# Sample attention of a hybrid layer: key pages turned in 32x32 blocks on VectorE, all of them in the stretch of prompt attention, values in the delta rule

## The chip, the cores and the metric

One core of one Trainium2 chip runs the whole program. The metric is the device time of one execution in microseconds. Fp32 data throughout; large weight matmuls are made of three matmuls of rounded parts.

## The reference

One layer of a macaron transformer (half a feed-forward, token mixing, half a feed-forward, adaLN modulation) for a prompt of 256 tokens and for 8 sequences of 4 new tokens that each have 2048 past tokens in a paged cache. Token mixing adds two head groups on the same input: a gated delta rule (4 heads of 128) and block attention (8 heads of 64). What the change touches is the attention of the new tokens and the order in which it stands beside the delta rule:

```python
def moba_sample(q, k, v, cache_k, cache_v, page_table):
    past = page_table.shape[1] * PAGE_SIZE          # 16 pages of 128
    ppb = MOBA_BLOCK // PAGE_SIZE                   # 2 pages to a block
    j = past // MOBA_BLOCK                          # 8 blocks
    l_own = own_block_logits(q, k_own, t, ..., slopes)
    k_full = cache_k[page_table[:, : j * ppb]].reshape(b, j, MOBA_BLOCK, h, hd)
    kmean = jnp.mean(k_full.astype(jnp.float32), axis=2)
    gate = jnp.einsum("bqhd,bnhd->bqhn", q.astype(jnp.float32), kmean)
    _, idx = lax.top_k(gate, 3)                     # per query and head
    ...
    l_sel = selected_logits(q, k_sel, t, idx, slopes)
    return attend_merged(l_sel, v_sel, l_own, v_own)   # one softmax over 3 blocks and the own 4 tokens
```

The kernel makes the logits of all 8 blocks, because different queries and heads choose different blocks, gets the gate from their sums, and sets the logits of unchosen blocks so low that their probabilities are 0. All 128 key pages and 128 value pages (256 KB each) are read.

## The kernel before, in words

Each engine has a program of its own, with semaphores between them; an engine runs its instructions in the written order, so the order in the text is the schedule. After the projections (`w_in`, 29 turns of a PSUM bank) the kernel runs:

- a short preparation: K and V rows of the tokens are transposed for the outputs, the block-diagonal queries `Qbd` built by ScalarE, the logits of the own tokens made (L972);
- **the key stretch**, 64 steps over `m`. The 8 sequences go in two halves `g`; a unit `n` is one block of 256 keys of four sequences, so 16 units, and `m = 4n + c` takes feature chunk `c`. Per step TensorE transposes 8 pieces of 128x128 (helper line L704) into two banks, ScalarE copies one bank (L1465), VectorE the other (L1855), and one step later four matmuls make logits (L1015). VectorE adds the bias and takes sums and maxima (L1795 to L1798). Between the steps, once a unit, stands one turn of prompt attention (`attention(s)`, one head a turn: scores, bias, maximum, exponential, transposes, values), and later the squares, sums and inverse roots of the delta rule's queries and keys;
- **the delta rule** in 128-token chunks, 9 problems (8 of the prompt, one for all new tokens): an opening (cumulated decays, rows, decay matrix `DT`, transposed keys `KB`, `KDc` and values `VB`, Gram matrices), seven levels of the triangular inverse (`P`, `XP`, `PX`, L1187, L1196, L1200) with the sample steps between them (`sample(l)`, L1161 for the products with the recurrent states `st`), then the last chain `W`, `U0`, `S1`, `V1`, `o0`, `o1`, `S2`, and the norm sums `rms`. At each of 17 places `values(n)` puts in one block of value pages of four sequences: probabilities (ScalarE), two transposes (L704), a copy (L1847) and 8 matmuls of 512 columns (L1055); own tokens L1061, gathering into the mixed input L1069. VectorE does nearly all PSUM copies of this part, the level masks (L1933) and the masking by decay. ScalarE issues the loads of the states (L1515) when the key stretch is over;
- the output projection (L1251) from `wo`, two halves of W_out.

Pages go through `page`: a table entry is loaded into a register (L533) and one DMA is issued (L534), half the pages by SP and half by POOL. Slots: 12 units of key pages (8 in `kv`, 4 in the last slot of `wring`), four quads of value pages in `kv`. The slots of `wring` hold weight tiles before and the delta rule's buffers during this time. W_out goes to `kv` when the last values but one are read (L607 to L610).

## Time and profile before

| | us |
|---|---|
| median of 3 runs (lowest, highest) | 928.0 (927.4, 933.94) |
| profiled execution | 927.22 |
| its span on the core | 925.6 |
| TensorE busy in the span | 859.5 |
| VectorE, ScalarE, POOL busy | 501.3, 304.6, 113.9 |

How to read it: a row of a stage or window gives the stretch, its length, then for PE (TensorE matmul), PEld (its weight loads), DVE (VectorE), ACT (ScalarE) and POOL the busy time and the number of instructions, then the granted TensorE clock as a share of full speed, the mean busy share of the 16 DMA engines and GB/s. A group row gives line, engine, operation, output and input with shapes, the count, busy time and mean ns of one, then the idle time before them and what ended it. Two records stand for one fp32 matmul and one for a transpose. A fp32 matmul pipelines with the next, so means of one are longer than the step between starts. A timeline row gives start, length and the merged instructions.

### The profile page before, as it was taken

Reading aid. Unit: us, or ns where it says so; the run is one execution under the profiler, and the core shown is the slowest. Engines: PE = TensorE matmul, PEld = TensorE weight load, DVE = VectorE, ACT = ScalarE, POOL = GpSimd, SP = SyncE. Lnnn points to the kernel's source line nnn. Section 1 sums busy time; section 2 is a strip of 40 time slices with the busy share of each in tenths; the row PEclk is TensorE's granted clock in tenths of the full one; section 3 lists DMA queues with packets and bytes.
Section 4 is the critical chain, followed back from the end, with each engine's and each line's share of the span. In section 5 each row is a group of like instructions: output and inputs, shape, how many; then the busy total and the mean of one; then the engine's idle time right before and its main releaser. Section 6 shows DMA issues by size and latency. Waiting matters only on the chain.

```text
span 925.6 us, 19660 instructions
## 1 busy us (share of the span) xinstructions
PE 859.5 (93%) x7464; PEld 751.7 (81%) x7464; DVE 501.3 (54%) x961; ACT 304.6 (33%) x499; POOL 113.9 (12%) x197
## 2 busy tenths in 40 slices
PE   4889999999999999999999848998899999999996
PEld 3789999998997999966656524665777999999996
DVE  1445454543355667566656566657446565544363
ACT  1333333332323336453434511000225334432331
POOL 2000000000021000132223223230130000000021
PEclk9999999999999999999999988999999999999999
DMA  9999979785755252378778698898391555434401
GB/s 323 370 307 357 308 255 312 253 320 185 300 199 182 92 182 59 125 243 268 230 232 289 205 369 289 296 333 311 87 338 57 167 182 176 145 137 156 159 1 51
DMA packets 122163, 204.83 MB, mean 221 GB/s; under 512 B 7548, under 2 KB 56982, under 8 KB 121970
## 3 DMA queue, kind: packets, MB, share of 16 engines
q1 hardware_dynamic: 104976, 163.08, 50.9%
q0 software_dynamic: 11648, 38.45, 12.4%
q10 hardware_dynamic: 5474, 2.39, 1.0%
q8 instruction: 46, 0.75, 0.3%
q14 instruction: 19, 0.16, 0.1%
HBM read 199.01 MB, written 4.88 MB: 220 GB/s over the span
## 4 chain that ended last, share of the span: by engine, by line
PE 83%; DVE 5%; DMA 4%; issue 2%; ACTq 2%; ACT 2%; POOL 1%; POOLq 1%; DVEq 0%; SPq 0%
PE bank L741 19%; PE bank L743 18%; PE bank L742 18%; PE bank L704 8%; PE bank L1015 3%; PE bank L1251 3%; PE bank L723 3%; PE bank L1055 2%; DMA kv<-in_cache_v 2%; ACTq L1515 2%; DMA wring<-in_w_ada 1%; DMA region<-in_x_sample 1%; DVE wring_rounded L1590 1%; PE bank L1200 1%; PE bank L1187 1%
## 5 line engine op out<-in xcount | busy, mean ns | idle before, releaser
L741 PE MATMUL bank<-hn_rounded,kv_rounded 128*128 128x288 f32 x928 | 276.7, 298 | 5.9 <-DVE wring_rounded L1590 4.1
L742 PE MATMUL bank<-xs_rounded,kv_rounded 128*128 128x288 f32 x928 | 274.4, 296 | 0.0
L743 PE MATMUL bank<-hn_rounded,wring_rounded 128*128 128x288 f32 x928 | 273.6, 295 | 0.0
L1590 DVE TENSOR_TENSOR wring_rounded<-wring,kv_rounded 128x1024 fp32r<-128x1024 f32 (+1 forms) x164 | 188.3, 1198 | 71.7 <-ACT kv_rounded L1311 71.6
L1311 ACT CAST kv_rounded<-wring 128x1024 fp32r<-128x1024 f32 (+1 forms) x164 | 158.5, 1026 | 162.0 <-PE bank L743 109.7
L741 PEld LDWEIGHTS bank<-hn_rounded,kv_rounded 128*128 128x128 f32 x928 | 174.4, 188 | 10.2 <-DVE wring_rounded L1590 4.7
L743 PEld LDWEIGHTS bank<-hn_rounded,wring_rounded 128*128 128x128 f32 x928 | 175.4, 189 | 0.0
L742 PEld LDWEIGHTS bank<-xs_rounded,kv_rounded 128*128 128x128 f32 x928 | 174.9, 189 | 0.0
L741 PE MATMUL bank<-region_rounded,kv_rounded 128*128 128x288 f32 x352 | 105.5, 300 | 1.6 <-DVE modT L1582 1.6
L742 PE MATMUL bank<-region_rounded,kv_rounded 128*128 128x288 f32 x352 | 104.6, 297 | 0.0
L743 PE MATMUL bank<-region_rounded,wring_rounded 128*128 128x288 f32 x352 | 104.2, 296 | 0.0
L1644 DVE TENSOR_TENSOR sgate<-sgate,bank 128x288 f32<-128x288 f32 x44 | 20.0, 454 | 131.1 <-PE bank L743 123.2
L741 PEld LDWEIGHTS bank<-region_rounded,kv_rounded 128*128 128x128 f32 x352 | 66.6, 189 | 2.4 <-DVE modT L1582 2.0
L743 PEld LDWEIGHTS bank<-region_rounded,wring_rounded 128*128 128x128 f32 x352 | 67.0, 190 | 0.0
L742 PEld LDWEIGHTS bank<-region_rounded,kv_rounded 128*128 128x128 f32 x352 | 66.8, 190 | 0.0
L1855 DVE COPY wring<-bank 128x512 f32<-128x512 f32 x64 | 44.1, 689 | 41.7 <-PE bank L704 40.7
L1465 ACT COPY wring<-bank 128x512 f32<-128x512 f32 x64 | 37.3, 584 | 70.4 <-PE bank L704 70.4
L1278 ACT ACTIVATE sgate<-bank 128x288 f32<-128x288 f32 x44 | 18.1, 412 | 104.5 <-PE bank L743 104.5
L704 PEld LDWEIGHTS bank<-const,kv 128*128 128x128 f32 x352 | 37.7, 141 | 17.3 <-ACT wring L1465 12.4
L704 PE MATMUL bank<-const,kv 128*128 128x128 f32 x352 | 47.9, 279 | 0.0
L641 POOL TENSOR_TENSOR xs<-h 128x288 f32<-128x288 f32 x21 | 14.0, 668 | 255.3 <-DVE h L1668 254.9
L534 POOL DMA_DIRECT2D kv<-in_cache_v x64 | 34.4, 537 | 84.5 <-issue 54.0
(275 smaller groups left out, 987.4 us busy)
## 6 DMA issues: line engine op xcount, KB each, us to landing
wring<-in_ffn_up SPq DMA_DIRECT2D x44, 1024.0 KB, 7.7
wring<-in_w_ada SPq DMA_DIRECT2D x36, 1024.0 KB, 10.9
wring<-in_ffn_down SPq DMA_DIRECT2D x16, 1024.0 KB, 7.3
kv<-in_cache_v SPq DMA_DIRECT2D x64, 256.0 KB, 4.9
kv<-in_cache_v POOLq DMA_DIRECT2D x64, 256.0 KB, 5.2
wring<-in_w_in SPq DMA_DIRECT2D x14, 1024.0 KB, 6.4
kv<-in_cache_k SPq DMA_DIRECT2D x44, 256.0 KB, 4.5
kv<-in_cache_k POOLq DMA_DIRECT2D x44, 256.0 KB, 4.8
```

The lines of the kernel that those rows point to most:

```text
L534: eng.dma_start(dst, cache[which][bass.ds(p, 1), :, :].rearrange("a p n -> (a p) n")).then_inc(landed, 16)
L704: return nc.tensor.transpose(out, in_, ident[0:n, 0:n])
L723: m = nc.tensor.matmul(out[32 * g:32 * g + 32, 0:P], cT[:, k, :], wring[:, slot, k, g * P:(g + 1) * P], start=(k == 0), stop=(k == KD - 1) ...
L741: nc.tensor.matmul(out, hi, rhs_hi, start=start, stop=False)
L742: nc.tensor.matmul(out, hi, rhs_lo, start=False, stop=False)
L743: return nc.tensor.matmul(out, lo, rhs_hi, start=False, stop=stop)
L1015: ins = mm(ps[4][32 * b4:32 * b4 + 32, 0:BLK], Qbd[:, c, 4 * (n // NBLK) + b4, :], ktb[:, c % 2, b4 // 2, (b4 % 2) * BLK:(b4 % 2 + 1) * BL ...
L1251: m = mm(ps[4 * (1 - g) + i][:, 0:TOK], wo[g][:, k, i * P:(i + 1) * P], mix[:, k, :], start=(k == 4), stop=(k == 3))
L1311: nc.scalar.copy(whiR[:, u % 2, c, :], wring[:, n % RING, c, :]).then_inc(s_whi, 1)
L1465: nc.scalar.copy(ktb[:, m % 2, 0, :], ps[2 * (m % 2)][:, :]).then_inc(s_ktA, 1)
L1590: v.tensor_tensor(wringR[:, slot, c, :], wring[:, slot, c, :], whiR[:, u % 2, c, :], ALU.subtract).then_inc(s_wlo, 1)
L1855: v.tensor_copy(ktb[:, m % 2, 1, :], ps[2 * (m % 2) + 1][:, :]).then_inc(s_ktD, 1)
```

## The change

- A **quad** is four pages of one sequence, 1 MB; there are 32 for keys and 32 for values. SP alone issues them, one table load for four entries. The first eight go to two free slots of `wring` and to `kv` as the projections release them, each later one into the slot of the quad four before it in `kv`.
- `keys_turned`: VectorE transposes a quad in place in 32x32 blocks. With query weights `W` laid out to match (a permuted spread of the queries by TensorE, masked per sequence by POOL), 16 matmuls give logits of one quad in a layout of head pair, key block, head and token on partitions. `logits_out`: ScalarE copies them from PSUM with block sums; POOL adds the bias, VectorE takes the block maxima. Gates and sums are added over partitions by a matmul with `same`.
- `transposed(b)`: 64 small matmuls with `pick` take the probabilities of one sequence, apart for both halves of the heads, and turn them; values are then 16 matmuls of 128 columns with 8 weight columns per quad.
- The order is a list of portions; all 32 key quads stand between the ten turns of prompt attention, four portions a turn, the value quads between steps of the delta rule, and the last five behind its norm sums.
- The delta rule's copies of rows, keys, and of the last chain go from VectorE to ScalarE, level masks, triangular mask, the products of queries and the clearing for the state products to POOL. Norms use one table of ScalarE (logarithm straight from PSUM).
- W_out goes to `wring` slots 0 and 1 behind the end of the delta rule; the tiles that come after it into these slots wait for its last readers. The bias constants shrink.

```python
# SP
+            for n in range(2 * QUADS):
+                if n < 8 and n % 2 == 0:
+                    sp.wait_ge(*released(("in", (3, 4, 5, 6)[n // 2])))
+                elif n >= 8:
+                    sp.wait_ge(*consumed(n - 4))
+                load_quad(n)        # one load of 4 table entries, 4 dma_starts of 256 KB
+            sp.wait_ge(s_gdn, 1)
+            for g in range(2):
                 for k in range(2):
                     sp.dma_start(wo[g][:, 4 * k:4 * k + 4, :], ...).then_inc(s_wo[g], 16)
-            first_k_steps(sp, 0); stream_rest(sp, 0)   # and the same on POOL
-            for g in (1, 0):
-                sp.wait_ge(s_PV, 32 - 2 * g)
# order of all engines
+        def portions():
+            out = []
+            for n in range(QUADS):
+                out.append(("K", n // NQ, n % NQ))
+                out += {17: [("G", 0)], 18: [("X", 0)], 20: [("X", 1)], 22: [("X", 2)], 24: [("X", 3)],
+                        26: [("R", 0)], 29: [("T", 0)], 31: [("T", 1)]}.get(n, [])
+            for n in range(QUADS):
+                b, q = n // NQ, n % NQ
+                out.append(("V", b, q))
+                if q == NQ - 1 and b + 2 < NB:
+                    out.append(("T", b + 2))
+                out += {1: [("G", 1)], 3: [("X", 4)], 5: [("X", 5)], 9: [("X", 6)], 13: [("X", 7)], 15: [("R", 1)]}.get(n, [])
+            return out + [("O", NB - 1)]
+        def turns(point):           # 4 portions at points 0 to 9, the rest over 10 to 33
+            def upto(i):
+                return 4 * i if i <= 10 else 40 + (len(PORTIONS) - 46) * (i - 10) // 23
# TensorE
+            def logits(b, q):
+                n = NQ * b + q
+                pe.wait_ge(s_X, n + 1)
...
+                for j in range(4):
+                    for c in range(4):
+                        m = mm(ps[5 + 2 * (b % 2)][32 * c:32 * c + 32, P * q:P * q + P], W[b % 2][:, j // 2, 2 * c + j % 2, :],
+                               keys[:, :, 4 * c + j, :], start=(j == 0), stop=(j == 3), tile_position=(0, 32 * c))
+            for s in range(HM + 2):
+                attention(s)
+                if s < 8:
+                    qk_sum(s)
+                attend(s)
# ScalarE, behind the key stretch
+            for part in (RSq, RSk):
+                fn(part, part, ACT.Exp, scale=-0.5).then_inc(s_rse, 1)
+            act.wait_ge(s_pav, 8)
             act.wait_ge(s_own, 1)
             for hh in range(HG):
                 act.dma_start(st[hh], a["state_gdn"][0, :, hh].rearrange("b k v -> k b v")).then_inc(s_st, 16)
# VectorE
+            def keys_turned(n):
+                dve.wait_ge(*quad_landed(n))
+                v.transpose(quad(n), quad(n)).then_inc(s_X, 1)
+            for s in range(HM + 2):
+                normalise(s)
+                biased(s)
...
+                attend(s)
```

## Rows read from the trace of the kernel before

**Rows 1.** Stages, 402.7 us to the output projection
```profile
402.70:529.40 126.70, 121.83 (x1116) 76.70 (x1115) 81.67 (x185) 57.85 (x126) 31.01 (x58) 1.00 0.73 238
529.40:566.70 37.30, 22.40 (x153) 11.56 (x153) 20.47 (x55) 5.63 (x15) 9.86 (x19) 0.82 0.96 324
566.70:664.50 97.80, 86.51 (x780) 61.19 (x776) 63.84 (x146) 7.65 (x21) 23.93 (x43) 0.98 0.75 266
```

**Rows 2.** Groups by line and shape, 402 to 530 us
```profile
L704 PE MATMUL bank<-const,kv 128*128 128x128 f32 x343 | 46.8, 279 | 0.0
...
L1855 DVE COPY wring<-bank 128x512 f32<-128x512 f32 x64 | 44.1, 689 | 41.7 <-PE bank L704 40.7
```

**Rows 3.** Waits of TensorE over the whole span
```profile
PE bank L704 <- ACT sgate L1278: 11.8, 1, 11.8
...
PE bank L704 <- ACT region L1278: 6.7, 1, 6.7
PE bank L1055 <- DMA kv<-in_cache_v: 6.7, 5, 2.4
```

**Rows 4.** ScalarE's queue in time, and its DMA queue, 530 to 665 us
```profile
540.82 11.50 ACTq L1515 DMA_DIRECT2D region<-in_state_gdn  x3
...
q10 hardware_dynamic: 4160, 2.10, 5.8%
```

**Rows 5.** Groups by line and shape, 402 to 530 us, nearest prices
```profile
L1780 DVE SCALAR_TENSOR_TENSOR wring<-const,bank 128x384 f32<-128x384 f32 x8 | 4.4, 554 | 1.3 <-PE bank L984 1.3
...
L1278 ACT ACTIVATE wring<-wring 128x128 f32<-128x128 f32 x8 | 3.3, 412 | 0.0
...
L1772 DVE TENSOR_SCALAR wring<-wring 128x256 f32<-128x256 f32 x8 | 2.8, 347 | 0.0
...
L1771 DVE TENSOR_SCALAR wring<-wring 128x128 f32<-128x128 f32 x8 | 2.3, 287 | 0.3
...
L1873 DVE COPY wring<-region 128x1152 f32<-128x1152 f32 x1 | 1.3, 1344 | 0.0
```

**Rows 6.** Timeline row (own logits) and line view (state matmuls)
```profile
399.35 1.49 PE L972 MATMUL bank<-region,adasb 128*32 128x32 f32 x64 [1.90 <-DVE wring L1759]
...
L1161 PE MATMUL bank<-region,wring x96: 272/273/297, 605.4 to 608.8; 128*32 128x128 f32 x96
```

**Rows 7.** Windows inside the opening and at level 0
```profile
536.00:546.00 10.00, 5.74 (x48) 2.68 (x44) 9.93 (x36) 1.87 (x5) 3.97 (x8) 1.00 1.02 370
546.00:556.00 10.00, 0.00 (x0) 0.00 (x0) 2.62 (x5) 0.10 (x1) 1.07 (x2) 0.53 1.07 358
...
576.00:578.50 2.50, 1.61 (x9) 0.28 (x9) 0.08 (x1) 0.00 (x0) 1.07 (x2) 0.76 1.01 396
```

**Rows 8.** SP's issues of the first four pages, 362 to 369 us
```profile
364.13 3.67 SPq L534 DMA_DIRECT2D wring<-in_cache_k  x4
...
L533 SPq TENSOR_LOAD <-ptab x4: 272/274/463, 363.2 to 366.8; - x4
...
L534 SPq DMA_DIRECT2D wring<-in_cache_k x4: 332/344/361, 364.1 to 367.5; - x4
```

**Rows 9.** Page slots by window; transposed probabilities, 529.4 to 664.4 us
```profile
566.70:664.50 97.80, 22.36 (x181) 4.45 (x177) 21.47 (x40) 0.98 0.75 266
...
L704 PE MATMUL bank<-const,sgate 128*128 128x128 f32 x30 | 6.1, 286 | 11.8 <-ACT sgate L1278 11.8
```

**Rows 10.** POOL's squares; VectorE's final scaling, its line view
```profile
L641 POOL TENSOR_TENSOR xs<-h 128x288 f32<-128x288 f32 x21 | 14.0, 668 | 255.3 <-DVE h L1668 254.9
...
L1671 DVE TENSOR_SCALAR hn<-h,pvec x8: 370/876/880, 885.8 to 917.1; 128x288 f32<-128x288 f32 x8
```

**Rows 11.** Loads of W_out, and the first projection matmul
```profile
L610 SPq DMA_DIRECT2D kv<-in_w_out x4: 368/448/508, 630.8 to 636.9; - x4
DMA to landing us min/median/max: 6.1/7.4/8.7
...
664.48 3.88 PE L1251 MATMUL bank<-hn,kv 128*128 128x288 f32 x15 [0.60 <-issue]
```

More of the change, by code:

```diff
@@ L527, in squared @@
+        PORTIONS = portions()
+        POINTS = 33
+        def turns(point):
+            def upto(i):
+                return 4 * i if i <= 10 else 40 + (len(PORTIONS) - 46) * (i - 10) // 23
+            return PORTIONS[upto(point):upto(point + 1)] if point < POINTS else PORTIONS[upto(point):]
         def squared(ni, c):
             return KD + (2 * KD - 3) * (ni - 1) + 2 * c + 1
[L531 to L534 removed]
@@ new lines, in win_turn, with left_bank, sum_bank, final_bank @@
+        def win_turn(q):
+            return q + (q >= AB_TURN)
+        def left_bank(turn):
+            if turn < CC:
+                return s_xc, turn + 1
+            if turn == AB_TURN:
+                return s_ab, 1
+            return s_zm, turn - CC + (turn < AB_TURN)
+        def sum_bank(ni):
+            return 4 if ni else 0
+        def final_bank(t, half):
+            return (4 + t, (7, 0, 1)[t])[half]
+        def probs(g):
+            return [range(0, 4), range(4, 8), range(8, 9)][g]
@@ L662, in _ @@
+            for point in range(29, POINTS + 1):
+                attend(point)
             pool.wait_ge(*copied(("S2",)))
@@ new lines, in transposed @@
+            def transposed(b):
+                pe.wait_ge(s_pe, b + 1)
+                if b:
+                    pe.wait_ge(s_PTe, b)
+                else:
+                    pe.wait_ge(s_ev, 7)
+                row = S[:, b].rearrange("p n k -> p (n k)")
+                for x in range(4 * NQ):
+                    for kb in range(4):
+                        m = mm(ps[5][32 * kb:32 * kb + 32, 32 * x:32 * x + 32], row[:, 32 * x:32 * x + 32], cst("pick")[:, 32 * kb:32 * kb + 32],
+                               start=True, stop=True, tile_position=(0, 32 * kb))
+                m.then_inc(s_PT, 1)
@@ new lines, in attend @@
+            def attend(point):
+                for what, b, *q in turns(point):
+                    if what == "K":
+                        logits(b, q[0])
+                    elif what == "G":
+                        gates(b)
+                    elif what == "R":
+                        sums(b)
+                    elif what == "T":
+                        transposed(b)
+                    elif what == "V":
+                        values(b, q[0])
+                    elif what == "O":
+                        gathered(b)
@@ new lines, in probs_transposed, with attend @@
+            def probs_transposed(b):
+                act.wait_ge(s_PT, b + 1)
+                if b >= 2:
+                    act.wait_ge(s_PV, NQ * (b - 1))
+                nc.scalar.copy(PT[b % 2], ps[5][:, :].rearrange("p (x n) -> p x n", x=4 * NQ)).then_inc(s_PTe, 1)
+            def attend(point):
+                for what, b, *q in turns(point):
+                    if what == "K" and q[0] == NQ - 1:
+                        logits_out(b)
+                    elif what == "X":
+                        exponentials(b)
+                    elif what == "T":
+                        probs_transposed(b)
@@ new lines, in attend @@
+            def attend(point):
+                for what, b, *q in turns(point):
+                    if what == "K":
+                        keys_turned(NQ * b + q[0])
+                        if q[0] == 1 and b:
+                            block_max(b - 1)
+                    elif what == "G":
+                        selection(b)
+                    elif what == "R":
+                        sums_out(b)
+                    elif what == "V" and q[0] == 2 and b:
+                        into_mix(b - 1)
+                    elif what == "V" and q[0] == NQ - 1:
+                        weighted(b)
+                    elif what == "O":
+                        into_mix(b)
```

861 lines of the change are left out of this document (422 added, 439 removed).

## Prediction

> **What bounds the kernel now.** I read the table of stages first. The change touches one third of the span, from the last projection at 391.6 us to the output projection at 664.5 us; the matmul stages on either side keep their instructions. After a short preparation [rows 1] cuts it into three: the key stretch with prompt attention between its turns (402.7 to 529.4, 126.7 us), the opening of the delta rule (37.3 us) and its levels with the value tiles between them (97.8 us). The reader should see that TensorE is busy for 121.8 of its 126.7 us in the key stretch and 86.5 of 97.8 us in the levels, while VectorE stands at 82 and 64 us. So TensorE is the bound, in order, with two holes. Next I read which groups fill the key stretch [rows 2]: 128-column transposes of keys through PSUM (46.8 us for the pages that lie in one of two rings) and the 64 copies of the transposed keys out of PSUM on VectorE (44.1 us), with as many on ScalarE. Then the waits of TensorE [rows 3]: 11.8 us at once on ScalarE in the opening, and 6.7 us on ScalarE late in the key stretch, where the norms of queries and keys take two table loads. The timeline of ScalarE tells why the first is there: from 540.8 us its queue issues the four loads of recurrent state, three of them in 11.50 us, and nothing behind them on ScalarE runs [rows 4]. They are 4160 small packets, 2.1 MB, which took 5.8% of the DMA engines' time over 135 us, or 7.8 us of all sixteen.
>
> **Key stretch: what goes.** All 512 PE transposes of key pages and both kinds of copies. A quad (four pages, 1 MB) is turned in 32x32 blocks by one VectorE instruction over 2048 columns, and 16 matmuls with 32 weight columns and 128 moving columns make its logits. No transpose by VectorE stands in the trace, so I bound it: a fp32 instruction from SBUF to SBUF at the slow slope costs 1.344 us for 1152 columns [rows 5], which makes 2.3 us for 2048; the fast slope is that of the scaling of probabilities, 0.347 us for 256 columns against 0.287 for 128 on the same page, about 1.2 us for 2048. I take 2.25 us (2.2 where one follows another), because nothing in the trace with a reordering runs at the fast slope; 1.2 us stays as the lower end, and 32 quads make a difference of 34 us. The Trainium skill, Vector Engine (DVE) Microarchitecture Reference, section 3.8, says that the transposing front-end sustains one element per cycle and lane; no run here shows it yet, and by it a quad would cost what I take.
>
> The matmul price comes from the state matmuls of the same shape: 64 instructions, the first start at 605.4 us and the last at 608.8 with 0.27 us of its own [rows 6], 57 ns each, so 0.91 us a quad. TensorE's work in the stretch falls by some 75 us, and **VectorE becomes the bound**. A full turn of prompt attention on it: four quads 8.8 us, one maximum over 512 logits 0.65, bias and two maxima 1.2 (the bias alone 0.554 [rows 5]). Before the bias it waits for TensorE, which is in order: last logits 1.0 and the next scores 1.1 us. Together 12.8 us. Turn 0 has no maximum and no such wait, 11 us. By the list of portions, turns 0 to 3 have four quads; turn 4 three and the selection (16 small dependent instructions, 4.2 us): 14.8; turn 5 has two quads, but two rounds of exponentials and one of copies put some 10 us on ScalarE; turns 6 and 7 three quads, 10.6 each; turn 8 9.2; turn 9 6.5. Sum: 11 + 38.4 + 14.8 + 10 + 21.2 + 9.2 + 6.5 = 111 us, with last logits and 3 us for crossings 115. The preparation grows by 2.7 us: the decay rows are transposed after keys and values, and VectorE empties V and convolution rows that much later. The start of the stretch is then 404 us and its end 519, **10 us earlier** than 529.4.
>
> **Is the DMA hidden there?** Eight quads are loaded before the stretch, the others follow in a ring of four. Four quads in 12.8 us are 328 GB/s; 370 GB/s over ten us were reached [rows 7]. All issues move to SP's queue, and each of 64 loads stands behind the wait for quad n-4. SP took 3.67 us for four pages, each with its own table load of 0.27 us; a DMA issue takes 0.33 us [rows 8]. One load of four entries should leave about 3.0 us a quad, below the 3.25 that VectorE needs. So I cost the move of the issues at nothing; VectorE's turns are the cover. The old cadence of 1.11 us a page (4.4 a quad) is the upper bound and a rival. POOL is freed of 128 issues and adds eight biases and the query weights, hidden behind the next turn.
>
> **Opening of the delta rule.** Now 37.3 us. After: two exponentials of norms on ScalarE and the last logits and copies behind the end of the stretch, 6.5 us; then the same four state loads, still ahead of everything the delta rule wants of ScalarE. At most four value quads compete with them, so I take 8 us, between 2 (issues of 0.4 us) and 15 (as now). Then decay rows 2.7, differences 1.9, exponential 1.3, and 18 scaled copies of keys, moved from VectorE to ScalarE: at 0.31 us from start to start, 5.6 (one alone is 0.412 [rows 5]); Gram matmuls and their last masking 5; the first level mask on POOL 1.2. Sum 32 us, **5 us less**. The mask by the triangle also moves to POOL, 2.4 us, hidden behind ScalarE's 5.6 us.
>
> **Levels with values.** [rows 9] gives what leaves: value matmuls 22.4 us; in both delta stretches together 6.1 us of transposed probabilities, two thirds of it here, 4; gathers and own rows, some 5. Of the 6.7 us of waits for value pages [rows 3] 4.4 lie here and go as well. What comes: 22 quads at 0.91 us, 20; five turnings of picked probabilities of 64 matmuls, 46 ns each by the own logits (32 in 1.49 us) [rows 6], 14.7; own values and gathers 2. Portions between the last steps fill some 4 us of waits. Level masks move to POOL: 0.668 us for 288 columns [rows 10] makes 1.1 us for 512, ready before the level wants them except for level 1, behind a clearing of 2304 columns: 2 us. From 97.2 to about 96 us.
>
> **Output projection: a new wait.** Until now W_out is loaded into free page slots, issued at 630.8 to 636.9 us and landed 7.4 us later [rows 11]; the projection starts 0.6 us after the last norm sums. After the change it lies in the ring that the delta rule uses, so SP waits for the end of the rule before it issues it, and TensorE waits for that. End of rule: logarithm, exponential and two products, 4.9 us behind the norm sums (now some 7, with two table loads); first half landed 8 us later. The last five value quads lie in this shadow. 12.9 instead of 0.6 us, **12.3 us more**, and some 1.5 us because the clock is low after the gap. SP's tile loads for the second feed-forward stand behind W_out, but their rounding is wanted only some 20 us later.
>
> **A rule on the ports.** The scaling of the final rows on VectorE takes 0.370 us at best and 0.876 in the middle, while POOL multiplies beside it [rows 10]. The Trainium skill, SBUF — State Buffer, section Who interferes with whom, says that such pairs exclude each other for a whole instruction. Most level steps on VectorE read one operand from PSUM and would not be held by that rule; a dozen at level 0 and at the norm products would, some 3 us in all. I put 3 us for crossings of all kinds.
>
> **Sum.** -10.4 (stretch ends) - 5 - 1.2 + 12.3 + 1.5 + 3 = about 0. The profiled execution took 927.2 us with 925.6 in its span; the median is 928.0. I predict 928. A difference within 1% (9 us) is about what this kernel's runs can't tell from none.
>
> **Rivals.** (1) Turned at the fast slope: 1.05 us less a quad. VectorE's full turn would be 8.6 us, but four quads at 350 GB/s need 12, so the DMA bounds the stretch from the fifth quad on: 24 quads in some 78 us plus the start, end at 502 to 505. About 911 us. With it go lesser gains of the same sign: the state loads issued in 2 us, or the values filling holes better. 0.30 in all. (2) TensorE stays busy for only some 40% of the key stretch and drops to 1.2 GHz, its lower level. For: after a wait of 2.4 us it was granted 0.76 of full speed (the stretch from 576 us), and 0.53 after 546 us. Against: from 536 to 546 us it was busy for 5.7 of 10 us in short pieces and kept 1.00, its 2.4 GHz [rows 7]. It decides once bursts and waits of 1.3 us count as idle; logits and scores on the turn's path double, 2 us for ten turns, and the opening starts slowly: 18 to 22 us, 948. 0.18. This is the slower end. (3) SP's issuing bounds: 4.4 us a quad, 24 quads from 421 us end the keys at 530, and 27 values at 4.4 instead of 3.6 us add 16 in the levels: some 27 us, 955. 0.14. (4) The change does not do what it says, because the key tiles don't fit between the turns: then TensorE waits out each turn and the times are those of the forecast, 0.38, or of (2). Nothing moves the keys out from the turns, so (4) gets no time of its own.
>
> The chances: forecast 0.38, (1) 0.30, (2) 0.18, (3) 0.14. Faster by over 1% is (1) less its small cases, 0.28; within 1% 0.37; slower 0.35. The range leaves out a tenth at each end: 906 to 958.
>
> **What would show it.** Transposes of 2.2 to 2.3 us, 32 of them; VectorE busy over 85% of the key stretch and the full turns near 13 us; key end at 519; SP's four issues in about 3 us; ScalarE's state loads still ahead of a hole on TensorE; waits for value pages small; W_out issued after the rule's last product and a wait of 6 to 12 us on it. Wrong would make it: another price of a transpose, a granted clock of 0.5 in the turns, or further waits between engines on this many crossings.

## The result and the profile after

The changed kernel takes **949.6 us** (median of 4 runs, 946.49 to 955.73) beside 929.4 us (927.4 to 933.94) for the kernel before in the same comparison: a ratio of 1.0218, 95% interval 1.0153 to 1.0284. It is 20 us slower; the forecast was 928. The profiled execution took 946.49 us with 944.4 us in its span, 18.8 more than the 925.6 of before.

I read the stages first. The rows are the windows of the profile after: start and end, length, busy time and count of TensorE's products and weight loads, VectorE, ScalarE and POOL, granted clock, DMA share, GB/s.

```profile
402.70:532.20 129.50, 87.68 (x1388) 58.14 (x1386) 96.34 (x111) 42.25 (x256) 15.04 (x23) 0.70 0.68 224
532.20:556.30 24.10, 18.91 (x368) 14.77 (x361) 16.23 (x39) 17.29 (x66) 9.09 (x7) 0.93 0.99 335
556.30:655.70 99.40, 92.71 (x1945) 79.64 (x1945) 42.34 (x98) 15.94 (x56) 27.35 (x24) 0.97 0.69 223
655.70:680.60 24.90, 10.67 (x181) 6.30 (x181) 3.74 (x6) 1.66 (x2) 0.00 (x0) 0.57 0.99 348
680.60:714.70 34.10, 34.07 (x128) 26.01 (x128) 11.02 (x25) 5.17 (x5) 10.69 (x13) 0.92 0.67 221
```

They are cut at the same instructions as [rows 1]: the first product of the cumulated decays (529.5 us before, 532.2 after), the first level product (566.7 and 556.3), the end of the norm sums (663.9 and 655.7), the first product of the output projection (664.5 and 680.6) and its last (695.8 and 714.7). So the 18.8 us stand in this account, read from one execution of each kernel:

| step | before | after | change | forecast |
|---|---|---|---|---|
| end of the key stretch | 529.5 | 532.2 | +2.7 | -10.4 |
| opening of the delta rule | 37.2 | 24.1 | -13.1 | -5 |
| levels to the end of the norm sums | 97.2 | 99.4 | +2.2 | -1.2 and 3 for crossings |
| norm sums to the projection | 0.6 | 24.9 | +24.3 | +12.3 |
| projection itself | 31.3 | 34.1 | +2.8 | +1.5 |

TensorE is busy for 87.7 of 129.5 us in the key stretch, where it was busy for 121.8 of 126.7: the transposes and their copies are gone as foreseen, and nothing was gained. Its clock there is 0.70 of full speed. The other conspicuous row is the fourth: TensorE busy for 10.7 of 24.9 us while the DMA engines are 0.99 busy. That row does not exist before.

**A turn of the key stretch** on VectorE, with the transposes of a quad in L1943 (first a row of the groups, then the timeline of 426 to 431 us; start, duration, instruction, and in brackets the idle time before it with its releaser):

```profile
L1943 DVE STREAM_TRANSPOSE kv<-kv 128x2048 f32<-128x2048 f32 x28 | 63.1, 2286 | 1.2 <-DMA kv<-in_cache_k 1.2
```

```profile
425.98 0.12 DVE L1920 RECIPROCAL wring<-wring 128x2 f32<-128x2 f32 x1
...
429.66 0.55 DVE L1930 SCALAR_TENSOR_TENSOR wring<-const,bank 128x384 f32<-128x384 f32 x1 [2.98 <-PE bank L1067]
```

```profile
DVE wring L1930 <- PE bank L1067: 17.3, 8, 3.0
...
DVE kv L1943 <- DMA kv<-in_cache_k: 1.2, 1, 1.2
```

The third fence is from VectorE's waits in the stretch (total, times, longest). VectorE waited 17.3 us in eight turns for the scores, up to 2.98 at a time, and only 1.2 us for pages. (In the kernels of experiments 1, 2 and 9, whose key stretch is the same, it waited 4.8, 3.5 and 2.8 us for pages.) In that gap TensorE does the last logits and the scores, at one clock or the other (timeline of TensorE, the ends of turns 0 and 1; the scores, L1067, are those of the next head):

```profile
413.50 1.08 PE L1104 MATMUL bank<-wring,adasb 128*32 128x128 f32 x32 [0.26 <-DVE wring L1943]
...
414.83 0.59 PE L1067 MATMUL bank<-region 64*128 64x256 f32 x2
...
426.11 1.94 PE L1104 MATMUL bank<-kv,adasb 128*32 128x128 f32 x32 [0.26 <-DVE kv L1943]
...
428.56 1.06 PE L1067 MATMUL bank<-region 64*128 64x256 f32 x2
```

**SP's queue.** Three quads (timeline of SP in three narrow windows), one row that joins 13 quads, the steps of its line L626, and SP's waits of the stretch:

```profile
421.58 1.88 SPq L630 DMA_DIRECT2D kv<-in_cache_k  x4
...
425.02 1.88 SPq L630 DMA_DIRECT2D kv<-in_cache_k  x4
...
428.46 1.88 SPq L630 DMA_DIRECT2D kv<-in_cache_k  x4
...
421.58 47.27 SPq L630 DMA_DIRECT2D kv<-in_cache_k  x52
```

```profile
L626 SPq FUSED_REGOPS  x112: 147/150/159, 420.4 to 533.0; - x112
L626 SPq SEQ_ASSERT  x112: 18/18/18, 420.6 to 533.2; - x112
L626 SPq TENSOR_LOAD <-ptab x28: 294/296/304, 420.1 to 531.9; - x28
```

```profile
SPq L626 <- PE bank L1104: 33.9, 8, 21.3
```

Four issues take 1.88 us, as [rows 8] let expect. But the next quad begins 3.44 us after the one before, not 3.0 (over the 13 quads 3.71 in the mean, twelve steps in 44.6 us, with two waits of 1.1 us together and some issues that took up to 0.8 us longer): between them stand the table load and, for each of its four page numbers, a test against its bounds (a register step of 0.15 us and an assertion, some 1.0 us in all with the gaps, as experiment 5 shows). Of the 28 quads that it issued in the stretch, the first four of values among them, SP waited before 8; without the first wait, 12.6 us in all. It was nearly a bound.

**The end.** SP's queue, W_out's issues with their landing, and TensorE and VectorE (timelines 655 to 690 us):

```profile
653.97 15.54 SPq L630 DMA_DIRECT2D kv<-in_cache_v  x15
669.56 4.16 SPq L641 DMA_DIRECT2D wring<-in_w_out  x4
```

```profile
L641 SPq DMA_DIRECT2D wring<-in_w_out x4: 432/510/2578, 669.6 to 671.1; - x4
...
DMA to landing us min/median/max: 8.3/11.6/15.1
```

```profile
658.91 1.36 DVE L2120 TENSOR_TENSOR hn<-xs 128x1152 f32<-128x1152 f32 x1
```

```profile
674.26 1.90 PE L1164 MATMUL bank<-kv,sgate 128*8 128x128 f32 x32 [1.50 <-DMA kv<-in_cache_v]
...
680.59 24.62 PE L1356 MATMUL bank<-hn,wring 128*128 128x288 f32 x89 [2.81 <-DMA wring<-in_w_out]
```

The rule ends at 660.3 us, 4.6 behind the norm sums as forecast. W_out is issued 9.3 us later, because SP stands behind the last value quads, and its first half arrives 10.9 us after that (TensorE starts at 680.6).

### The profile page after: what moved, and what is told of

Its sections match the earlier page's. It is cut to its first block, busy times and chain, and to the rows that moved or that the text cites. A ratio compares the mean times of both kernels' runs of the same rounds, so it can differ in the third digit from the quotient of the medians.

```text
span 944.4 us, 22701 instructions
## 1 busy us (share of the span) xinstructions
PE 840.3 (89%) x9312; PEld 761.5 (81%) x9312; DVE 490.2 (52%) x830; ACT 308.2 (33%) x715; POOL 94.3 (10%) x118
## 4 chain that ended last, share of the span: by engine, by line
PE 47%; DVE 11%; SPq 3%; DMA 3%; issue 2%; POOL 1%; ACT 1%; ACTq 0%; DVEq 0%
PE bank L817 11%; PE bank L819 11%; PE bank L818 11%; DVE kv L1943 6%; PE bank L1356 4%; SPq L630 2%; PE bank L1104 2%; PE bank L1164 1%; PE bank L1288 1%; DMA wring<-in_w_out 1%; PE bank L1296 1%; PE bank L780 1%; DMA kv<-in_cache_v 1%; SPq L626 1%; PE bank L1300 1%
## 5 line engine op out<-in xcount | busy, mean ns | idle before, releaser
L1104 PE MATMUL bank<-kv,adasb 128*32 128x128 f32 x896 | 44.2, 360 | 36.4 <-DVE kv L1943 36.4
L1104 PEld LDWEIGHTS bank<-kv,adasb 128*32 128x32 f32 x896 | 32.4, 144 | 49.3 <-DVE kv L1943 47.7
L1943 DVE STREAM_TRANSPOSE kv<-kv 128x2048 f32<-128x2048 f32 x28 | 63.1, 2286 | 1.2 <-DMA kv<-in_cache_k 1.2
L799 PE MATMUL bank<-wring,cT 128*32 128x128 f32 x1152 | 37.2, 285 | 7.4 <-DMA wring<-in_w_ada 7.4
L674 POOL TENSOR_TENSOR xs<-h 128x288 f32<-128x288 f32 x21 | 14.9, 710 | 285.3 <-DVE h L1821 284.9
L799 PEld LDWEIGHTS bank<-wring,cT 128*32 128x32 f32 x1152 | 32.4, 114 | 10.4 <-issue 9.8
## 6 DMA issues: line engine op xcount, KB each, us to landing
wring<-in_w_ada SPq DMA_DIRECT2D x36, 1024.0 KB, 10.9
```

What stands on the lines that cost most here:

```text
L799: m = nc.tensor.matmul(out[32 * g:32 * g + 32, 0:P], cT[:, k, :], wring[:, slot, k, g * P:(g + 1) * P], start=(k == 0), stop=(k == KD - 1) ...
L1104: m = mm(ps[5 + 2 * (b % 2)][32 * c:32 * c + 32, P * q:P * q + P], W[b % 2][:, j // 2, 2 * c + j % 2, :], keys[:, :, 4 * c + j, :], start= ...
L1943: v.transpose(quad(n), quad(n)).then_inc(s_X, 1)
```

## The experiments

All are made from the kernel after unless said otherwise. Each is given by its median and by its ratio to the kernel before from the same comparison, since the medians of before lay between 928.7 and 931.8 us; the kernel after stands at 1.0218. Positions in time are those of one profiled execution each. Four kernels with an identical key stretch (after, 1, 2 and 9) had 124.6 to 127.0 us from the first bias to the end of the last transpose, mean 125.9; the kernel after is the shortest of them, and differences of one or two microseconds there say nothing. The opening of the delta rule scatters more: from the first product of the cumulated decays to the first level product it took 23.1 to 31.4 us in kernels whose opening is the same.

**1 and 2: the end.** Values earlier; then W_out in the page slots as well.

```
- return ... 40 + (len(PORTIONS) - 46) * (i - 10) // 23
+ return ... min(len(PORTIONS), 40 + (len(PORTIONS) - 40) * (i - 10) // 19)
second kernel, besides:
- wo = [wring[:, g] for g in range(2)]
+ wo = [kv[:, 4 * g:4 * g + 4].rearrange("p a b n -> p (a b) n") for g in range(2)]
- sp.wait_ge(s_gdn, 1)                       # ahead of both halves
+ sp.wait_ge(s_PV, 30 + 2 * g)               # ahead of each half
```

The rounding into the page slots then waits for the projection's products, as before the change.

> The five value quads and the last gather that TensorE does behind the delta rule are spread over its levels, so that all values are done some points before the rule ends; W_out stays in the ring that the rule uses. Theory A (the forecast's own term: the projection waits for the rule's end and then for the first half of W_out): the 20.3 us between the rule's end and the first product of the output projection become 8 to 10, the rule ends 3 to 6 us later, and the kernel comes to 942 to 946 us. Theory B (the gap is the queue: SP issues W_out only behind the last value quads, and those wait for slots and for the DMA engines, busy 0.99 of the time from 651.8 to 680.6 us): the gap becomes 8 to 10 as well, and the two differ on the next kernel alone, but SP's first issue of W_out moves from 9.3 us behind the rule's end to within 0.5 us of it. Theory C (the levels have no room for more values): the rule ends 10 us or more later and the time stays at 949.

> As the kernel before it, and W_out goes into the four page slots as soon as the last values have been read, as it did before the change; SP no longer waits for the rule before it. If the place of W_out costs what theory A says, another 8 to 10 us go and the projection starts within 2 us of the rule's end: 933 to 938 us. If the DMA engines are what is short around the rule's end (theory B in its strong form), W_out still lands 6 us or more behind the rule's end and the time is 940 to 944.

Measured: 961.6 us (1.0349, interval 1.0282 to 1.0416) and 944.4 us (1.0151, 1.0089 to 1.0213). In the first, SP's wait and the gap on TensorE:

```profile
SPq L641 <- DVE hn L2120: 24.7, 1, 24.7
```

```profile
678.32 2.21 PE L1341 MATMUL bank<-wring,const 128*128 128x288 f32 x8 [0.98 <-ACT wring L1383]
697.00 8.38 PE L1356 MATMUL bank<-hn,wring 128*128 128x288 f32 x26 [16.48 <-DMA wring<-in_w_out]
```

In the second:

```profile
678.86 26.43 PE L1355 MATMUL bank<-hn,kv 128*128 128x288 f32 x108 [0.79 <-ACT wring L1382]
```

The first misses all three expectations in its size: the norm sums ended at 680.5 instead of 655.7 us. Of these 24.8 us, 4.6 were there before the opening began (536.8 instead of 532.2), up to where the edit changes nothing; the opening took 5.6 us more and the levels 14.7. So the five value quads and two gathers, spread over both, went with 20 us, not 3 to 6; where the kernel after has them, behind the rule, they stand in the shadow of the wait for W_out. Theory C comes nearest, and even it did not foresee a loss of 12 us. The second is above theory A's 933 to 938 us too: W_out was there in time (first issue at 658.7), but the norm sums ended at 678.1. But the pair shows the forecast's term by itself: with nothing queued ahead, W_out is issued at the rule's end (685.1), its first half is there 11.9 us later, and TensorE idles 16.5 us; with W_out in the page slots that idle time is 0.8 us and the kernel 17 us faster (2.5 of them already at the end of the norm sums, in the two profiled executions). The place of W_out costs 16 us, of which the late values hide a part.

**3: a warm TensorE.**

```
+ def warm(count, n):
+     ...
+     for _ in range(count):
+         mm(ps[6][:, 256:384], ones, ident, start=True, stop=True)
  logits of a quad: + if q < NQ - 1: warm(6, n)      behind qk_sum: + warm(8, 4 * s)
```

> Nothing of the computation changes. In the key stretch TensorE gets six 128x128 products with a constant result behind the logits of every quad but the last of a turn (up to the sums of probabilities), and eight behind the attention of every turn, into an unused part of a bank. Theory 1 (the lower clock of TensorE, 0.70 in the mean of the key stretch, doubles the last logits and the scores, which stand between VectorE's last transpose of a turn and its next bias): granted clock 0.95 or more in the stretch, the gap of 3.7 us between them becomes 2.1, the stretch is 8 to 12 us shorter and the kernel comes to 938 to 942 us. Theory 2 (the order: what costs is that they stand there at all): at most 3 us less. Theory 3 (pages land late, SP or DMA): no change, 949.

Measured: 949.5 us (1.0210, 1.0156 to 1.0264). The granted clock rose to 0.93 (404 to 518 us), and the last transpose ended at 530.5 instead of 528.0 us. The timeline of TensorE says why this run cannot decide:

```profile
435.76 1.60 PE L1115 MATMUL bank<-const 128*128 128x128 f32 x12
437.30 1.08 PE L1104 MATMUL bank<-kv,adasb 128*32 128x128 f32 x32
```

Six fp32 products are twelve instructions and take 1.53 us, the logits 1.01: 2.54 us a quad, while VectorE delivers one every 2.21. The fillers had become the bound. Experiments 7 and 8 repeat it with half of them.

**4: scores ahead of the last portion.** The two score products move into a function of their own, and TensorE calls it for the next head before the turn's fourth portion.

```
- for what, b, *q in turns(point):
+ for i, (what, b, *q) in enumerate(turns(point)):
+     if point < HM - 1 and i == 3:
+         scores(point + 1)
```

> Nothing of the computation changes. TensorE computes the next head's scores ahead of the last portion of a turn instead of behind it, so VectorE finds them ready when its fourth transpose ends. Theory 2 (order): the 3.7 us between VectorE's last transpose and its next bias become 0.7 in the turns of four quads, some 20 us less in the stretch where the pages keep up; four quads in 11 us are 380 GB/s, so the DMA may take back half: 930 to 940 us. Theory 1 (clock alone) allows the same but with the clock still at 0.5 to 0.7. Theory 3 (pages land late): VectorE waits for pages by as much as it no longer waits for TensorE, 946 to 949.

Measured: 945.7 us (1.0174, 1.0099 to 1.0249). From the first bias to the last transpose it takes 121.2 us, 3.4 fewer than the kernel after. In the time of the kernel the gain is not clear of noise (the two intervals overlap), and in the profiled execution it is gone by the first level product, which starts at 556.0 us instead of 556.3. The waits of VectorE:

```profile
DVE kv L1949 <- DMA kv<-in_cache_k: 7.0, 5, 3.2
DVE wring L1936 <- PE bank L1066: 5.5, 4, 3.0
```

The wait for the scores fell from 17.3 to 5.5 us, the one for pages rose from 1.2 to 7.0. This is what theory 3 asked for, in half of the size: right behind TensorE's part of the turn stood the supply of pages.

**5: SP without the bounds test, then with the scores early, and with fixed pages.**

```
  _, pages = nc.values_load_multi_w_load_instructions(..., min_val=0, max_val=NPHYS - 1,
+     skip_runtime_bounds_check_because="the table holds pages of the pool")
fixed pages: - bass.ds(pages[x], 1)   + (4 * m + x) % NPHYS:(4 * m + x) % NPHYS + 1, and no table load
```

> The kernel after, but SP does not test the four page numbers of a quad against their bounds after loading them: twelve register steps of 0.8 us in all go from between two quads, whose issue otherwise stays. Theory S (SP's queue bounds the supply of pages: where it waits for nothing it takes 3.44 us from quad to quad): 2.65 us from quad to quad; in the key stretch VectorE's turns still hold, 0 to 4 us less; the last ten value quads, 41 us from the first issue to the last, take 33, and the output projection starts 5 to 8 us earlier: 940 to 944 us. Theory D (the DMA engines bound the values at the end, 0.99 busy from 651.8 to 680.6 us): the projection starts within 2 us of before, 947 to 949 us.

> As the kernel before it, and the next head's scores ahead of the last portion of a turn. Alone the order of the scores took 4 us from the key stretch, because VectorE then waited 7 us for pages. Theory S: the page waits of VectorE fall under 2 us, turns of four quads take 11.5 to 12.5 us instead of 14.1, the last key transpose ends 12 to 16 us before that of the kernel after (528.0 us), and the time is 926 to 934 us. Theory D: the waits for pages stay at 5 us or more and the key transposes end at 521 to 524: 936 to 942 us.

> Leaves out the look-up of page numbers: SP loads fixed pages, so many and as large as before, without a table load, a bounds test or a register. SP then needs some 2 us for the four issues of a quad. With the scores ahead of the last portion. Theory S: as the kernel without the bounds test or up to 5 us faster. Theory D: the same as that kernel within 1 us, VectorE still waiting for pages.

Measured: 943.1 us (1.0150, 1.0128 to 1.0173), 933.7 us (1.0045, 1.0027 to 1.0063) and 933.4 us (1.0040, 1.0020 to 1.0060). SP in the first of them, in two narrow windows of its timeline, and its waits:

```profile
427.94 1.88 SPq L631 DMA_DIRECT2D kv<-in_cache_k  x4
...
430.34 1.92 SPq L631 DMA_DIRECT2D kv<-in_cache_k  x4
```

```profile
SPq L626 <- PE bank L1105: 56.5, 14, 23.3
```

The pitch is 2.40 us, so the test is worth 1.04 (my expectation had 0.8 and twelve steps; there are eight). SP now waits 33.2 us behind its first wait (415 to 520 us), where the kernel after has 10.9. From the first bias to the last transpose: 119.5 us, 115.1 with the scores early, 114.6 with fixed pages. With fixed pages SP needs as little as 1.80 us from quad to quad, so nothing more is to be had from SP. The projection starts 8.6 us earlier (672.0 instead of 680.6), but 5.2 of them stand at the end of the norm sums already; behind these it is 21.5 instead of 24.9 us. Theory S is borne out in the key stretch, where the test is worth 5 us alone and the order of the scores 4.4 more. How it acts there is shown in part: with the test alone gone no wait for pages is left (1.2 to 4.8 us in the four kernels named above), but VectorE's waits for TensorE fell as well, those for the scores from 17.3 to 15.2 and those for the attention's result from 5.1 to 2.4, at a granted clock of 0.75 instead of 0.69 (404 to 518 us). No run takes these apart. In the time of the kernel the interval without the test still overlaps that of the kernel after at its edge; with the scores early it lies clear below.

**6: all three.** No bounds test, scores early, and the end of experiment 2 with the values spread to the 31st point (`// 22` in place of `// 19`).

> No bounds test, scores ahead of the last portion, all values done by the point before the rule's last (instead of five quads behind it), W_out into the page slots behind the last values. If SP's pitch was what made the earlier values cost 23 us of the rule's time: the rule ends 8 to 12 us later than in the kernel with the first two changes alone, the projection starts within 4 us of the rule's end, and the kernel takes 914 to 924 us, less than both kernels of this case. If the values in the levels cost TensorE time and DMA time as such: 930 to 936 us.

Measured: **924.8 us, ratio 0.9947, interval 0.9929 to 0.9965**: about half a per cent faster than the kernel before, and 2.7% faster than the one after. Its own rows (timeline of TensorE):

```profile
655.04 2.21 PE L1347 MATMUL bank<-wring,const 128*128 128x288 f32 x8 [0.97 <-ACT wring L1389]
658.04 4.36 PE L1362 MATMUL bank<-hn,kv 128*128 128x288 f32 x17 [0.79 <-ACT wring L1389]
```

The projection starts at 658.0 us, 0.8 behind the norm sums. The time lies 1 us above the range that I gave; the rule ends 12.0 us later than with the first two changes alone (661.8 and 649.8), the upper end of the 8 to 12 expected.

**7 and 8: fillers that fit.** Three products behind a quad, four behind the attention of a turn; on the kernel after, and on the one without the bounds test. Before them I had run six and eight fillers without the test.

> No bounds test on SP, and the fillers on TensorE of the earlier run (six products behind the logits of a quad, eight behind the attention of a turn). With fillers alone the granted clock of the key stretch rose from 0.70 to 0.91 and nothing was gained, which theory S explains by SP's pitch of 3.44 us. If the clock is a bound of its own once SP is quicker (theory 1 behind S): turns of four quads 12 to 12.7 us instead of 13.1 to 13.8, last key transpose ending at 518 to 521 instead of 524.5, 936 to 939 us. If the clock costs nothing here: 942 to 944, the transposes ending at 524 or later, the fillers themselves in the way.

> The kernel after with half the fillers: three products behind the logits of a quad, four behind the attention of a turn. Six took 1.53 us beside logits of 1.01, which makes 2.54 us a quad where VectorE delivers one in 2.21: the fillers themselves came late and hid what the clock gives. Three take 0.77, 1.78 in all. Theory 1 (the clock is a bound of the stretch of its own): granted clock 0.9 or more, VectorE's wait before the bias 1.4 instead of 2.2 to 3.0 us, key transposes ending 5 to 10 us before 528.0, 938 to 944 us. Theory S (SP's pitch stands right behind it): the waits for TensorE fall, those for pages rise by as much, 945 to 949 us.

> The same fillers without SP's bounds test. Clock and SP both bounds, one behind the other: here the gain of the clock shows in full, turns of four quads 12.4 to 12.7 us instead of 13.1 to 13.8, key transposes ending at 518 to 521 instead of 524.5 us, 937 to 940 us (the kernel without the test alone: 943.1). Clock no bound: 942 to 944.

Measured: the six and eight without the test 945.8 us (1.0185, 1.0126 to 1.0245), not faster than without fillers (1.0150; the intervals overlap), as the reason above lets expect; three and four on the kernel after 945.3 us (1.0140, 1.0095 to 1.0186); without the test 939.7 us (1.0089, 1.0058 to 1.0121; without fillers 1.0150). Windows of 404 to 518 us, after, then three and four fillers, then the same without the test:

```profile
404.00:518.00 114.00, 76.71 (x1029) 49.95 (x1027) 88.57 (x104) 39.92 (x239) 13.17 (x19) 0.69 0.67 220
```

```profile
404.00:518.00 114.00, 86.47 (x1237) 65.18 (x1241) 87.40 (x106) 37.96 (x223) 14.22 (x23) 0.89 0.68 218
```

```profile
404.00:518.00 114.00, 87.86 (x1327) 66.21 (x1328) 90.89 (x109) 39.88 (x239) 14.54 (x22) 0.90 0.71 236
```

```profile
429.31 0.56 DVE L1941 SCALAR_TENSOR_TENSOR wring<-const,bank 128x384 f32<-128x384 f32 x1 [1.39 <-PE bank L1068]
```

The last row is VectorE's, without the test: the wait of 2.98 us is 1.39. From bias to bias the first four turns take 12.0, 14.2, 14.1 and 14.9 us in the kernel after; with fillers 12.0, 12.6, 15.6 and 14.5 (VectorE waits for pages in the third); without the test 12.0, 13.1, 13.3 and 13.8; with both 12.0, 12.6, 12.6 and 13.1. Of these four kernels only the one with both has the turn that the forecast made, 12.8 us. The fillers have a price too: at the turn of the selection VectorE waits 4.55 and 3.81 us for the scores, instead of 2.98. To the last transpose the fillers gain 1.8 us with the test and 0.7 without, against a scatter of 1; in the time of the kernel they gain more, 0.6% without the test, where the intervals do not overlap. Where the rest of that lies isn't settled, and these traces can't tell: the profiled executions with fillers are the longer ones (spans of 947.4 and 939.5 us beside 944.4 and 936.0), with openings of the rule of 29.4 and 31.4 us beside 24.1 and 23.9.

**9: the end alone.** The end of experiment 6 on the kernel after.

> The kernel after with only the end changed: all values done by the point before the rule's last, W_out into the page slots behind them; bounds test and scores as in the kernel after. Tells what the place of W_out and the five values behind the rule are worth by themselves, and closes the account of the kernel of 924.8 us (after less 6.5 for the test, 9.4 for the scores, 8.9 for the end). If the three add: 939 to 942 us. If the end's gain needs SP's shorter pitch: 944 or more.

Measured: 936.7 us (1.0048, 1.0016 to 1.0080): 1.7% of the time, some 16 us, more than expected. The changes do not add: beside the shorter pitch and the early scores the same end brings 9 us.

**10: half a transpose.** On the kernel of 933.7 us; `v.transpose(quad(n)[:, 0:1024], quad(n)[:, 0:1024])`.

> Leaves out the transposition of the second half of each quad: 1024 columns instead of 2048 on VectorE, all else (no bounds test, scores ahead of the last portion, the same pages and products) as in the kernel of 933.7 us. If VectorE bounds the key stretch there, a quad costs 1.1 us less and the stretch (405.2 to 519.1 us) ends 20 to 35 us earlier. If the ring of four quads and the supply of pages bound it (issue, landing, transpose, logits, then the next issue into the slot): 3.0 us a quad and more remain, the stretch ends 5 to 15 us earlier, and VectorE waits for pages by most of what it saved.

> The fastest kernel so far (924.8 us) with four fillers behind the logits of a quad and four behind the attention of a turn. If TensorE's clock still costs in the loop of issue, landing, transpose and logits: the key stretch ends 2 to 4 us earlier and the kernel takes 920 to 923. If not: 924 to 927.

Measured: one run, 926.4 us. From the first bias to the last transpose it takes 99.4 instead of 115.1 us, 15.7 less for the 35 us that VectorE no longer works, and between the two cases expected (the stretch began 2.8 us later; the decay differences start at 521.3 instead of 534.1). Its waits for pages rise to

```profile
DVE kv L1950 <- DMA kv<-in_cache_k: 14.7, 10, 2.8
```

So VectorE's transposes still bound a part of the stretch, and the ring of four quads takes over at once when they shrink. The kernel of 924.8 us with four fillers (second expectation) took 926.6 us (0.9972, 0.9937 to 1.0006): no gain. That this is because the scores no longer stand in VectorE's way is my reading; no run shows it.

## Why the prediction was wrong

The range of 906 to 958 held the time; the forecast of no change did not hold. Two steps failed by 13 and 12 us, one by 8 the other way.

- **"So I cost the move of the issues at nothing; VectorE's turns are the cover"**, on 3.0 us a quad for SP, is the first step that failed. SP took 3.44 (3.71 in the mean over 13 quads). I had subtracted three table loads from 3.67 us [rows 8], but that is the time from the first issue to the end of the fourth and holds three of the four intervals; the base was the 4.4 us that I used as the upper bound, and less 0.8 it gives 3.6. The bounds tests, 1.0 us of it, were not in my reckoning at all. Four quads at that pitch are 14 to 15 us, beyond a turn of 12.8. Taking out the test alone gave 5 us of the stretch, and with it and the scores early it is 9.5 us shorter. Rival (3) named this mechanism and priced it at 27 us by the old cadence; the measured pitch lies between.
- **The granted clock** is the second half of the same step. VectorE's last transpose of a turn is followed by TensorE's last logits and scores, which I put at 2.1 us. That is what they take at 2.4 GHz, the upper level; in the turns at 0.66 to 0.77 of the clock VectorE waited up to 2.98 us instead of 1.39. Rival (2) had the mechanism and the place right: logits 1.08 us become 1.94. Its price, 18 to 22 us, was wrong by far: VectorE's waits for the scores exceed 1.39 by 7.0 us in all seven turns, and half the fillers gained 2 us in the stretch and 0.6 to 0.8% in the kernel, 6 to 7 us, of which only the smaller is clear of noise. That the result lies at its 948 us is an accident. Against it I had held that 5.7 busy of 10 us had kept the full clock [rows 7]; from 470 to 490 us TensorE was busy for 14.8 of 20 us and had 0.50. Busy time at the lower level is nearly twice as long for the same work, so the one row could not be held against the other.
- **By turns** the 13.1 us are: turns 0 to 3 5.8 more than the 49.4 of the forecast; the turn of the selection 18.4 instead of 14.8, of which 2.0 are its wait for the gate sums and some 1.6 the clock; turns 5 and 6 0.5 more; from the eighth bias to the end of the stretch 34.0 instead of 30.3; less 0.6 for the start.
- **"12.3 us more" for W_out** is the other failed step, and what failed is the sentence that the last five value quads lie in its shadow. They lie ahead of it in SP's queue. The chain behind the norm sums took 4.6 us (4.9 forecast), then W_out was queued for 9.3, then it landed in 10.9 instead of 8, on DMA engines 0.99 busy with value pages and the states going out. 24.9 us for the 12.9 of the sum. Experiment 1 shows that even without the queue it is 16.5.
- **The opening** came out 8 us better. I had two norm exponentials of 1.2 us each and the last logits ahead of the state loads; the exponentials run beside them, since ScalarE works while its queue issues (timeline of ScalarE; the exponentials stand ahead of the loads in its program):

```profile
532.40 0.40 ACTq L1612 DMA_DIRECT2D region<-in_state_gdn  x1
532.82 1.17 ACT L1383 ACTIVATE hn<-hn 128x1152 f32<-128x1152 f32 x1
532.83 3.05 ACTq L1612 DMA_DIRECT2D region<-in_state_gdn  x2
...
535.90 2.97 ACTq L1612 DMA_DIRECT2D spare<-in_state_gdn  x1
```

  The loads themselves took 6.5 us, within the bounds of 2 and 15 and near the 8 that I took; [rows 4] had 15.0 with the fourth. In the other kernels with this opening they took 4.5 to 10.9 us, and the opening 23.1 to 31.4 with 24.5 in the middle, so this execution is a usual one, but the 8 us do not hold in each. The 18 scaled copies took 4.7 us (5.6 forecast), and VectorE's gates and choice of blocks for the second half, which the sum did not have here, stand beside and behind them, 543.3 to 550.4 us, on the chain that ends last.
- **The levels** were right in their sum, +2.2 where -1.2 and 3 for crossings were put, and that was luck: the parts were not. Turning the probabilities cost 7.3 us busy and 3.2 of stalls instead of 14.7, value quads 24.3 for 23 of them instead of 20 for 22, and the waits for value pages, which I had let go, stayed at 4.4 us.
- **Right too**: a transpose of 2048 columns costs 2.21 us from start to start (2.25 and 2.2 forecast), all 32. The Trainium skill, Vector Engine (DVE) Microarchitecture Reference, section 3.8, has one element per cycle and lane for it, and the trace agrees: half the columns take 1.12 us (experiment 10), so a further column costs 1.06 ns. No row shows how long a cycle is.
- **Crossings of VectorE and POOL** were put at 3 us, at level 0 and the norm products; the mask by the triangle on POOL, 2.4 us, was put as hidden. It was not. A product of 256 columns on VectorE with both inputs in SBUF took 2.46 us where its neighbours take 0.42, and ended 0.28 us behind that mask:

```profile
544.45 0.42 DVE L1962 TENSOR_TENSOR region<-region 128x256 f32<-128x256 f32 x1
544.90 2.46 DVE L1963 TENSOR_TENSOR region<-region,const 128x256 f32<-128x256 f32 x1
```

```profile
544.58 2.50 POOL L730 TENSOR_TENSOR wring<-wring,const 128x1024 f32<-128x1024 f32 x1 [6.52 <-ACT wring L1383]
```

  That is what the Trainium skill, SBUF — State Buffer, section Who interferes with whom, states. The product of 1152 columns at 535.1 us shows the same: 2.77 us beside a POOL product of 2.63, where one of this size alone takes 1.36 (658.91 above). Both stand on the chain of work that ended last (chain from 530 to 562 us):

```profile
535.13 2.78 DVE wring L2048
...
544.90 2.46 DVE region L1963
```

  They take 1.4 and 2.0 us more than alone. Not all of it is lost. The first had the state loads close beside it: ScalarE came free of them only at 538.9 and went on at 539.05, so it cost next to nothing. The second held the masking of the Gram matrices: VectorE began it at 550.6, their first products had begun at 548.8, so at most 1.9 us are lost there. The kernel of experiment 4 and the first of experiment 5 show both pairs again, at 2.77 and 2.78 us and at 2.45.

What stays open: where the fillers' gain beyond the key stretch lies; why five value quads and two gathers went with 20 us of opening and levels in experiment 1, when the products of a quad take 1.06 us; and how the pitch of SP acts on VectorE's waits for TensorE. Pages, levels and the order of both are interleaved there, and no run took them apart.

## What to carry to other kernels

When a change moves issues to one queue, write down every step of that queue between two issues, bounds tests of loaded indices included, and compare the pitch with the period of the work it feeds; a bound a few per cent behind the first one can take over what an improvement gains, and the waits show it (here those for the scores fell by 11.8 us and those for pages rose by 5.8). A load that must wait for a late event also waits for all that its queue holds ahead of it: give it a place in memory that comes free early (with the values moved to suit, 16 us here). And look at what an engine that is no longer the bound answers in the path of the one that is: TensorE's logits took 1.94 instead of 1.08 us at the lower clock. Taking the scores out of the way by order brought 1.0% on the kernel without the test, keeping TensorE busy with fillers 0.6%. Last, work that is moved to POOL is not hidden only because POOL has time: look at what VectorE does beside it (a product of 0.42 us took 2.46 here, on the chain that ended last).

## What the hardware showed that I had not expected

- Testing four page numbers against their bounds on SP took 1.04 us a quad (eight steps): the pitch was 2.40 us without it and 3.44 with it.
- An fp32 product of 128 by 128 ran as two instructions and took 0.255 us, 0.128 for each of them, so six as fillers cost 1.53 us. Three behind each quad and four behind each attention went with a granted clock of 0.89 instead of 0.69 in the stretch.
- ScalarE went on computing while its queue held issued loads of 3 us (rows of 532.8 us above), because the two exponentials stand ahead of them in its program; the instruction behind the last issue waited 3.89 us, until that issue was over.
- A VectorE product with both inputs in SBUF took 2.46 instead of 0.42 us, and another 2.77 instead of 1.36, beside products of POOL of 2.50 and 2.63 us.
